# A two-layer decoder trunk on one core: the second stage dealt out to 24 slots, keys opened while their item is projected

## The chip, the cores and the metric

The kernel runs on one core of one Trainium2 chip. The metric is the device time of one execution in microseconds (us). An engine's name stands for itself: PE (matrix multiply), DVE (vector), ACT (scalar), POOL (GpSimd), SP (issues DMAs).

## The reference, cut to what matters

The second stage of the kernel is the gated DeltaNet of layer 0: a projection, a short causal convolution with SiLU, and a chunked delta rule over 8 heads. Sixteen meta tokens form a chunk of their own ahead of 2048 real tokens.

```python
proj = rmsnorm(h, norm_g) @ w_in
qkv = silu(causal_depthwise_conv(proj[..., :QKV_W], conv_w));  z = proj[..., QKV_W:...]
q, k = l2norm(q) * dk ** -0.5, l2norm(k)          # 8 heads, 128 wide
# per chunk of c tokens (16 meta tokens, then chunks)
tmat = eye(c) + where(strict, beta * (k @ k.T) * gam, 0)
u, w = triangular_solve(tmat, [v * beta, k * beta * exp(gcum)])
qk = (q @ k.T) * gam
def step(s, ...):                                  # one chunk after the other
    v_new = u_c - w_c @ s
    o_c = qd_c @ s + qk_c @ v_new
    s = s * dl_c + kd_c.T @ v_new
o = rmsnorm(o, o_norm) * silu(z);  return o @ w_out
```

Output projection, shared keys and values, the window attention of layer 1 and the final norm follow in the third and fourth stage, which the change doesn't touch.

## The kernel before

The program has four stages, one behind the other. The second, `gated_deltanet`, works on 32 **items**: 4 groups of 512 tokens times 8 heads. Items 0 to 7 also carry their head's meta chunk (a second `Pass`, of one chunk, ahead of the main one of four). It runs as a software pipeline of 34 **steps**. In step `it` PE projects item `it`; the passes `a` of item `it - 1` are **opened**; the passes `b` of item `it - 2` are **closed**. Steps 32 and 33 have nothing to project.

The names that the text uses:

- *Projection*: 8 units of 24 matmuls (two halves of 264 tokens, for keys, values, queries, gate in this order: `f` = 0 to 3), 192 in a step. The fp32 product is made of three fp32r ones, so each weight is split: ACT writes the high part (`split_high`), POOL the low part (`split_low`). ACT copies each unit out of PSUM (`evacuate`), DVE convolves it in four taps and bounds it (`convolve`, parts 0 to 4), ACT forms the sigmoid in three activations, POOL multiplies (`silu`) into `kT`, `vT`, `qT`, `zT`.
- *Opening*: `tok` transposes keys, queries and values (12 transposes on PE, L1103); `kk` and `kq` are the products; ACT squares and takes logarithms for the norms; DVE writes `k_dec`, `nU` (the strictly lower part), `v_s`, `qk`.
- *The rows*: DVE inverts the 16x16 diagonal blocks of `nU` row by row (`solve_row`, i = 1 to 15; a product and a reduction each, then the copy `p_Xbt`). The blocks come and go through DRAM: SP stores `nU` (`low_dram`), loads the blocks (`p_blk`); behind row 15 it stores 8 block tiles (L641) and loads the whole inverse `p_X`, `p_Xt` (L647, L649).
- *Levels*: `left` 0 to 2 and `right` 0 to 2 on PE, with DVE and ACT between, join the blocks to the inverse of 128x128. `left` 0 waits for the loaded inverse.
- *Recurrence*: `ks`, `wr`, `out` for each of 4 chunks, a chain PE, DVE (`p_r`), PE, ACT (`p_w`), PE, DVE (`p_state`).
- *Norm and close*: mean square on DVE, logarithm and scale on ACT (`p_on`, L808), four transposes on PE (L1188), product on DVE (`p_og`), a store.

`schedule` deals all that to **slots**, the same list on all engines. In a slot an engine first does its stages and then its share of projection, taps, sigmoids, splits or rows. Before, the list of a step with one pass each is: `tok`, `kk`, `left` 0, `right` 0, `kq`, `left` 1, `right` 1, `left` 2, `right` 2, the twelve of the recurrence, `norm`, `close`: 23 slots, all with about 8 or 9 projection matmuls. Weights are split as their units end. Every engine runs its own list in order and waits on semaphores. PE's `tok` has three waits, of which the first is for the SiLU of the queries:

```python
pe.wait_ge(silu_done, NF * p.item + 3)
```

The 8 PSUM banks are two for the projection and `k`, `v`, `l`, `t`, `c`, `q`. The outputs of the recurrence stand in `t` and `l`, which the levels use too, so `left` 0 of the next item waits until they are read.

## Time and profile before

| | us |
|---|---|
| median of 3 runs | 3182.96 (3181.33 to 3186.96) |
| the profiled execution | 3186.96 |
| its span, first to last instruction | 3185.1 |
| PE busy | 2614.5 (82%) |
| DVE busy | 1619.3 (51%) |
| ACT busy | 1227.2 (39%) |
| POOL busy | 864.6 (27%) |

The page has busy times over the whole span; the second stage's matmuls are L1083 to L1188, and its first projection matmul starts at 137.2. Items follow each other at a constant pace in a long stretch, so the windows and timelines below are cut at their borders. A number in square brackets behind a row is the time for which the engine sat idle before it, and what released it.

### The profile page before, as it was taken

What the parts mean: (1) busy time and instruction counts of PE and PEld (TensorE: products, weight loads), DVE (VectorE), ACT (ScalarE), POOL (GpSimd) and SP (SyncE); (2) the same over time, 40 slices, a digit from 0 to 9 for tenths busy, and PEclk for the clock granted to TensorE, in tenths of its full rate; (3) what the DMA queues carried; (4) which work ended last, traced back from release to release, by engine and by line L of the source; (5) the groups of instructions that cost most, each with busy time, mean ns of one, the idle gap of its engine ahead of it and who ended that gap; (6) DMA issues with size and microseconds to landing.
All of it is one profiled execution on the core that took longest, in us unless ns stands there. A gap on an engine that the chain in (4) does not pass through costs nothing. (4 is left out here: it accounts for less than half of the span.)

```text
span 3185.1 us, 51348 instructions
## 1 busy us (share of the span) xinstructions
PE 2614.5 (82%) x17497; PEld 2330.2 (73%) x17497; DVE 1619.3 (51%) x3652; ACT 1227.2 (39%) x3466; POOL 864.6 (27%) x700
## 2 busy tenths in 40 slices
PE   5577777878787878788787755999995899999997
PEld 4477777778787878777787734888883687888785
DVE  4367676565665656565666523222223444444442
ACT  4244444444444444444444323333332323323232
POOL 0143333333333333333333200000001233223231
PEclk8689998988898889898898757999997999999998
DMA  9632222322223322222222133333334222122111
GB/s 250 184 123 65 72 68 72 115 69 65 70 63 93 99 71 62 72 69 73 70 64 75 35 97 126 129 126 115 112 116 154 86 75 74 60 66 72 61 61 42
DMA packets 250075, 284.27 MB, mean 89 GB/s; under 512 B 72082, under 2 KB 188770, under 8 KB 249986
## 3 DMA queue, kind: packets, MB, share of 16 engines
q1 hardware_dynamic: 208866, 257.73, 26.2%
q10 hardware_dynamic: 41120, 25.37, 2.7%
q8 instruction: 54, 0.88, 0.1%
q14 instruction: 35, 0.29, 0.0%
HBM read 199.71 MB, written 83.33 MB: 89 GB/s over the span
## 5 line engine op out<-in xcount | busy, mean ns | idle before, releaser
L1083 PE MATMUL p_psp<-xg,p_whi 128*128 128x264 f32 x4096 | 890.3, 305 | 21.3 <-POOL p_wlo L1022 21.3
L1083 PEld LDWEIGHTS p_psp<-xg,p_whi 128*128 128x128 f32 x4096 | 685.7, 199 | 23.9 <-issue 18.3
L1083 PE MATMUL p_psp<-xg,p_wlo 128*128 128x264 f32 x2048 | 618.4, 302 | 0.0
L1022 POOL TENSOR_TENSOR p_wlo<-p_wraw,p_whi 128x512 fp32r<-128x512 f32 x260 | 368.3, 1433 | 300.0 <-ACT p_whi L731 299.9
L1083 PEld LDWEIGHTS p_psp<-xg,p_wlo 128*128 128x128 f32 x2048 | 403.9, 197 | 0.5
L863 DVE SCALAR_TENSOR_TENSOR p_acc<-p_proj,p_taps,p_acc 128x528 f32<-128x528 f32 x288 | 281.5, 977 | 9.2
L2142 PE MATMUL p_psq<-p_wq,p_hT 128*128 128x512 f32 x768 | 216.7, 420 | 38.4 <-DVE p_wq L2083 28.3
L1587 PE MATMUL p_psh<-p_wo,p_o 128*128 128x512 f32 (+1 forms) x816 | 198.1, 402 | 26.0 <-DVE p_wo L1557 22.1
L884 DVE TENSOR_TENSOR p_prod<-p_Xb,p_blk 32x4 f32<-32x4 f32 (+13 forms) x448 | 201.5, 450 | 3.9
L1587 PEld LDWEIGHTS p_psh<-p_wo,p_o 128*128 128x128 f32 (+1 forms) x816 | 150.3, 186 | 67.4 <-issue 19.4
L2142 PEld LDWEIGHTS p_psq<-p_wq,p_hT 128*128 128x128 f32 x768 | 140.5, 196 | 73.3 <-issue 23.2
L742 ACT ACTIVATE p_proj<-p_psp 128x264 f32<-128x264 f32 x256 | 99.5, 389 | 245.0 <-PE p_psp L1083 234.8
L2142 PE MATMUL p_pso<-p_wo,p_oT 128*128 128x512 f32 x768 | 189.6, 400 | 5.1 <-DVE p_oT L2037 5.1
L1569 POOL TENSOR_TENSOR p_o<-p_oraw,p_o 128x1024 fp32r<-128x1024 f32 (+1 forms) x17 | 38.8, 2280 | 508.7 <-ACT p_o L1411 508.7
L1587 PE MATMUL p_psz<-p_wk,p_hT 128*128 128x512 f32 x768 | 176.7, 389 | 0.0
L2142 PEld LDWEIGHTS p_pso<-p_wo,p_oT 128*128 128x128 f32 x768 | 142.5, 190 | 37.1 <-DVE p_oT L2037 8.8
L1103 PE MATMUL p_psk<-p_ident,p_kT 128*128 128x128 f32 x136 | 35.3, 398 | 162.7 <-POOL p_qT L1039 158.2
L1587 PEld LDWEIGHTS p_psz<-p_wk,p_hT 128*128 128x128 f32 x768 | 144.2, 188 | 29.9
L731 ACT ACTIVATE p_whi<-p_wraw 128x512 fp32r<-128x512 f32 x260 | 156.5, 620 | 11.2 <-DVE p_og L981 6.4
L1103 PEld LDWEIGHTS p_psk<-p_ident,p_kT 128*128 128x128 f32 x136 | 22.5, 198 | 171.4 <-issue 99.9
L1890 ACT ACTIVATE p_logits<-p_logits,p_top 128x144 f32<-128x144 f32 x256 | 102.6, 402 | 80.0 <-DVE p_top L1998 79.9
L2246 PEld LDWEIGHTS p_psq<-p_v,p_pT 128*128 128x128 f32 x992 | 119.2, 192 | 16.5 <-issue 11.7
(271 smaller groups left out, 4943.3 us busy)
## 6 DMA issues: line engine op xcount, KB each, us to landing
p_wraw<-w_a_in SPq DMA_DIRECT2D x130, 512.0 KB, 3.7
xg<-xT_dram SPq DMA_DIRECT2D x8, 2112.0 KB, 13.2
hT_dram<-p_hT SPq DMA_DIRECT2D x32, 512.0 KB, 2.9
p_hT<-hT_dram SPq DMA_DIRECT2D x32, 512.0 KB
p_x<-x_in SPq DMA_DIRECT2D x16, 512.0 KB, 4.9
xT_dram<-p_hi ACTq DMA_DIRECT2D x16, 512.0 KB, 6.4
xT_dram<-p_lo ACTq DMA_DIRECT2D x16, 512.0 KB, 7.0
p_grow<-rows_dram SPq DMA_DIRECT2D x32, 256.0 KB, 3.7
```

The lines of the kernel that those rows point to most:

```text
L731: nc.scalar.activation(w_hi[:, slot, cols], w_raw[:, slot, cols], ACT.Copy).then_inc(hi_ready, 1)
L742: nc.scalar.activation(proj[:, f % 2, 3 + half_ * HALF:3 + (half_ + 1) * HALF], ps_p[half_][:, 0:HALF], ACT.Copy).then_inc(proj_read, 1)
L863: nc.vector.scalar_tensor_tensor(a, p[:, part:part + GW], w, a, ALU.mult, ALU.add).then_inc(tap_done, 1)
L884: link(nc.vector.tensor_tensor(t3, x3[:, 0:i, 0:i].rearrange("p j c -> p c j"), b3[:, 0:i, i].unsqueeze(1).to_broadcast([rows, i, i]), ALU ...
L1022: nc.gpsimd.tensor_tensor(w_lo[:, slot, cols], w_raw[:, slot, cols], w_hi[:, slot, cols].bitcast(f32), ALU.subtract).then_inc(lo_ready, 1)
L1083: ins = nc.tensor.matmul(ps_p[half_][:, 0:HALF], (w_hi, w_lo)[i][:, f % 2, kc * P:(kc + 1) * P], xg[:, g % 2, j, kc, half_ * HALF:(half_ + ...
L1103: last = nc.tensor.transpose(ps[:, bank_of[c]], t[:, cols[c]], ident[:])
L1569: nc.gpsimd.tensor_tensor(o_s[1][:, :, 0:rows], o_raw[:, :, 0:rows], o_s[0][:, :, 0:rows].bitcast(f32), ALU.subtract).then_inc(o_lo, 1)
L1587: last = nc.tensor.matmul(out, stationary[i][:, kc, 0:rows], moving(j, kc), start=kc == 0 and n == 0, stop=kc == KC - 1 and n == 2)
L1890: last_ = nc.scalar.activation(logits[:, s_, :], logits[:, s_, :], ACT.Exp, bias=top[:, s_:s_ + 1], accum_out=den[:, s_:s_ + 1])
L2142: ins = nc.tensor.matmul(banks[b][:], stationary[i][:, kc, :], weights[j][:, kc, b * FB:(b + 1) * FB], start=kc == 0 and n == 0, stop=kc = ...
L2246: last_ = nc.tensor.matmul(ps_q[b][:, cols], pT[:, g % 2, x, n * P:(n + 1) * P], v[:, slot, kvh * HD:(kvh + 1) * HD], start=False, stop=g ...
```

## The change

- The step now has three items: `p` (item `it`) has its **keys** opened in the very step in which it is projected: `tokK`, `kk`, `kdec`, `low`, `tokV`, `vs`, and rows 1 to 7 of its solve. `a` (item `it - 1`) gets `tokQ`, `kq`, `qk`, rows 8 to 15 and the levels. `b` (item `it - 2`) gets recurrence, norm, close, and `store` as a stage of its own.
- 24 slots in a fixed order with tables: the recurrence of `b` comes first (slots 0 to 11), the levels of `a` in slots 12 to 17, close in 16. `FILL` gives the projection matmuls of each slot. Meta passes get slots of their own with no fill, ahead of slots 0, 2, 12 and 22.
- PSUM: outputs have two banks of their own (`o0`, `o1`), levels keep `l` and `t`; keys and values share `k`, queries and `kq` go through `l`. The close transposes go into `o0`.
- Weights: `w_hi` and `w_lo` hold all four `f`; `SPLIT` places the splits. `X` becomes one buffer, `cur` too, with the last decay kept in `e_last`; `states` holds 8 heads.
- `tok_ps`, `grown` are split into one semaphore for each operand.

```diff
@@ gated_deltanet
-        w_hi = sb("p2_whi", [P, 2, D], f32r)
+        w_hi = sb("p2_whi", [P, NF, D], f32r)
...
-        o_of = lambda c: (ps_t, ps_l)[c % 2][:, c * P:(c + 1) * P]
+        ps_o = (ps_o0, ps_o1)
+        o_of = lambda p, c: ps_o1[:, P:2 * P] if p.meta else ps_o[c % 2][:, c * P:(c + 1) * P]
+        ps_close = lambda p: ps_o1 if p.meta else ps_o0
...
+        FILL = (8, 9, 6, 8, 9, 8, 4, 10, 8, 8, 10, 8, 3, 2, 3, 5, 2, 9, 12, 12, 13, 13, 9, 13)
+        TAPS = {7: (0, 0, (0, 1)), 8: (0, 0, (2, 3)), 9: (0, 0, (4,)), 16: (0, 1, (0,)), 17: (0, 1, (1,)),
+                18: (0, 1, (2, 3)), 19: (0, 1, (4,)), 20: (0, 2, (0, 1)), 21: (0, 2, (2, 3)), 22: (0, 2, (4,)),
+                1: (1, 3, (4,))}
+        SILU = {11: (0, 0), 21: (0, 1), 0: (1, 2), 3: (1, 3)}
+        SPLIT = {5: (0, 3, 0), 6: (0, 3, 1), 7: (1, 0, 0), 8: (1, 0, 1), 14: (1, 1, 0), 15: (1, 1, 1),
+                 21: (1, 2, 0), 23: (1, 2, 1)}
+        ROWS_P = {19: (1, 2), 20: (3,), 21: (4,), 22: (5, 6), 23: (7,)}
+        ROWS_A = {0: (8, 9), 1: (10,), 2: (11,), 3: (12,), 4: (13,), 5: (14,), 6: (15,)}
...
+            if b:
+                if b[0].meta:
+                    for stage in ("ks", "wr", "out"):
+                        insert(0, (stage, b[0], 0))
...
+                for c in range(TPG):
+                    for n, stage in enumerate(("ks", "wr", "out")):
+                        put(3 * c + n, stage, main, c)
+                put(12, "norm", main, 0)
+                put(16, "close", main, 0)
...
+                for s, stage in ((2, "tokQ"), (6, "kq"), (9, "qk")):
+                    put(s, stage, main, 0)
+                for level in range(LEVELS):
+                    put(12 + 2 * level, "left", main, level)
+                    put(13 + 2 * level, "right", main, level)
...
+                for q in p:
+                    put(10, "gates", q, 0)
+                for s, stage in ((12, "tokK"), (13, "kk"), (13, "kdec"), (14, "low"), (22, "tokV"), (23, "vs")):
+                    put(s, stage, main, 0)
...
+                if stage == "tokK":
+                    pe.wait_ge(silu_done, NF * p.item + 1)
...
                 elif stage == "left":
                     if index == 0:
                         pe.wait_ge(inv_in[par], 32 * (p.turn + 1))
-                        if not (isinstance(b[0].chunk, int) and b[0].chunk == 0):
-                            pe.wait_ge(o_read, b[0].chunk)
+                        pe.wait_ge(qk_ready, k + 1)
...
-                        pe.wait_ge(norm_ready, 2 * k + 1)
+                    pe.wait_ge(q_squared, k + 1)
```

**PE, the border of two steps, before** (L1188 is close, L1103 `tok`; L1083 the projection):

```order
L1188 MATMUL p_psv<-p_ident,p_on 128x128 x4
L1083 MATMUL p_psp<-xg,p_whi 128x264 x2
L1083 MATMUL p_psp<-xg,p_wlo 128x264
L1083 MATMUL p_psp<-xg,p_whi 128x264 x2
L1083 MATMUL p_psp<-xg,p_wlo 128x264
L1083 MATMUL p_psp<-xg,p_whi 128x264 x2
L1083 MATMUL p_psp<-xg,p_wlo 128x264
L1103 MATMUL p_psk<-p_ident,p_kT 128x128 x4
L1103 MATMUL p_psq<-p_ident,p_qT 128x128 x4
L1103 MATMUL p_psv<-p_ident,p_vT 128x128 x4
```

**PE, slots 11 to 14 of the last projecting step, after** (L1205 `left`, L1164 `tokK`, L1222 `right`, L1172 `kk`, L1214 the transposes of `p_X`, L1146 the projection):

```order
L1146 MATMUL p_psp<-xg,p_whi 128x264 x2
L1146 MATMUL p_psp<-xg,p_wlo 128x264
L1205 MATMUL p_psl<-p_X,p_nU 128x64 x4
L1164 MATMUL p_psk<-p_ident,p_kT 128x128 x4
L1146 MATMUL p_psp<-xg,p_whi 128x264 x2
L1146 MATMUL p_psp<-xg,p_wlo 128x264
L1222 MATMUL p_psl<-p_half,p_Xt 128x64 x4
L1172 MATMUL p_psc<-p_kT 128x128 x4
L1146 MATMUL p_psp<-xg,p_whi 128x264 x2
L1205 MATMUL p_psl<-p_X,p_nU 128x64 x4
L1214 MATMUL p_pst<-p_ident,p_X 128x128 x4
L1146 MATMUL p_psp<-xg,p_wlo 128x264
```

The 12 transposes no longer stand together at a step's start; `left` 0 and the keys' transposes of a younger item now follow the recurrence, and the close has moved behind two levels.

**DVE, from row 15 on, before** (the last steps, where no convolution stands between; L888 is the copy that ends the rows, L966 `p_state` of the last chunk, L970 the mean square):

```order
L884 TENSOR_TENSOR p_prod<-p_Xb,p_blk 32x225
L886 TENSOR_REDUCE p_Xb<-p_prod 32x15
L888 COPY p_Xbt<-p_Xb 32x256
L966 SCALAR_TENSOR_TENSOR p_state<-p_state,p_cur,p_psc 128x128
L970 SCALAR_TENSOR_TENSOR p_oms<-p_oss,p_obias 128x4
```

**DVE, the same rows after** (slots 6 to 9 of a step; L952 is the copy):

```order
L1028 TENSOR_TENSOR p_r<-p_psc,p_vs 128x128
L948 TENSOR_TENSOR p_prod<-p_Xb,p_blk 32x225
L950 TENSOR_REDUCE p_Xb<-p_prod 32x15
L952 COPY p_Xbt<-p_Xb 32x256
L925 TENSOR_SCALAR p_acc<-p_proj,p_taps 128x528
L927 SCALAR_TENSOR_TENSOR p_acc<-p_proj,p_taps,p_acc 128x528
L1033 SCALAR_TENSOR_TENSOR p_state<-p_state,p_elast,p_psc 128x128
L927 SCALAR_TENSOR_TENSOR p_acc<-p_proj,p_taps,p_acc 128x528 x2
L1028 TENSOR_TENSOR p_r<-p_psc,p_vs 128x128
```

Row 15 stood ahead of the last chunk's `p_state`, at the end of a step; now it stands behind `p_r` of the third chunk, in slot 6, six slots ahead of the `left` 0 of the same step that needs the inverse.

## Rows read from the trace of the kernel before

**Rows 1.** Windows of PE over the second stage: stretch, us, busy (matmuls), clock, DMA.

```profile
267.30:545.40 278.10, 222.22 (x1690) 0.93 0.24 67
545.40:600.90 55.50, 45.57 (x338) 0.91 0.24 67
600.90:659.20 58.30, 45.53 (x331) 0.88 0.42 137
659.20:712.30 53.10, 41.56 (x320) 0.90 0.24 67
712.30:1020.00 307.70, 249.58 (x1920) 0.89 0.24 69
1020.00:1075.50 55.50, 44.10 (x321) 0.84 0.45 142
1075.50:1791.40 715.90, 579.43 (x4480) 0.90 0.24 68
1791.40:1873.00 81.60, 55.36 (x228) 0.54 0.08 24
```

**Rows 2.** Timeline of PE, item 1233.43 to 1284.57: start, us, matmuls [idle before].

```profile
1233.43 1.12 PE L1103 MATMUL p_psk<-p_ident,p_kT 128*128 128x128 f32 x4 [4.77 <-POOL p_qT L1039]
...
1277.45 0.66 PE L1188 MATMUL p_psv<-p_ident,p_on 128*128 128x128 f32 x4 [4.03 <-ACT p_on L808]
...
1284.57 0.47 PE L1103 MATMUL p_psk<-p_ident,p_kT 128*128 128x128 f32 x1 [4.87 <-POOL p_qT L1039]
```

**Rows 3.** Windows, all engines, the same item: PE, PEld, DVE, ACT, POOL busy; clock.

```profile
1233.43:1284.57 51.14, 41.40 (x320) 39.84 (x321) 32.13 (x79) 23.62 (x69) 19.02 (x15) 0.90 0.24 69
```

**Rows 4.** Windows of PE: the granted clock behind stalls, here and behind one at 328.

```profile
1228.10:1233.40 5.30, 0.57 (x3) 0.50 0.49 148
1233.40:1238.20 4.80, 4.76 (x26) 0.57 0.22 50
328.03:331.00 2.97, 2.97 (x14) 0.50 0.04 11
331.00:333.60 2.60, 2.60 (x17) 0.62 0.68 197
```

**Rows 5.** Timeline of DVE, the same item: the end of its rows.

```profile
1271.75 1.63 DVE L884 TENSOR_TENSOR p_prod<-p_Xb,p_blk 32x225 f32<-32x225 f32 x1
1273.42 0.38 DVE L886 TENSOR_REDUCE p_Xb<-p_prod 32x15 f32<-32x225 f32 x1
1273.83 0.92 DVE L888 COPY p_Xbt<-p_Xb 32x256 f32<-32x256 f32 x1
```

**Rows 6.** Timeline of POOL at that place.

```profile
1271.22 3.30 POOL L1022 TENSOR_TENSOR p_wlo<-p_wraw,p_whi 128x512 fp32r<-128x512 f32 x2
```

**Rows 7.** Timeline of SP, DMA issues behind those rows (x4 are four copies).

```profile
1275.06 1.43 SPq L641 DMA_DIRECT2D inv_dram<-p_Xb  x4
1276.54 1.87 SPq L641 DMA_DIRECT2D inv_dram<-p_Xbt  x4
1280.60 0.39 SPq L647 DMA_DIRECT2D p_X<-inv_dram  x1
1281.03 0.51 SPq L649 DMA_DIRECT2D p_Xt<-inv_dram  x1
```

**Rows 8.** Line 649, the load of the inverse: issue to landing.

```profile
DMA to landing us min/median/max: 3.2/3.4/4.8
```

**Rows 9.** Timeline of DVE in the last steps, where POOL is idle.

```profile
1828.35 0.53 DVE L884 TENSOR_TENSOR p_prod<-p_Xb,p_blk 32x225 f32<-32x225 f32 x1
...
1829.32 0.36 DVE L888 COPY p_Xbt<-p_Xb 32x256 f32<-32x256 f32 x1
```

**Rows 10.** Timeline of PE in the last steps.

```profile
1839.01 1.97 PE L1128 MATMUL p_psl<-p_X,p_nU 128*128 128x64 f32 x8 [5.51 <-DMA p_Xt<-inv_dram]
...
1854.84 0.80 PE L1166 MATMUL p_psc<-p_state,p_kg 128*128 128x128 f32 x2
...
1871.85 1.11 PE L1188 MATMUL p_psv<-p_ident,p_on 128*128 128x128 f32 x4 [2.30 <-ACT p_on L808]
```

More of the change, by code:

```diff
@@ L464, in gated_deltanet @@
         solved = sem("p2_solved")
+        scaled = sem("p2_scaled")
         left_ps = sem("p2_left_ps")
@@ new lines, in last_two, with finish, run @@
+        def last_two(step):
+            for it in (ITEMS - 2, ITEMS - 1):
+                step(it, it % 2, *three(it, it % 2, it // 2, False, False, False), (True, it < ITEMS - 1))
+        def finish(step):
+            _, a, b = three(ITEMS, 0, ITEMS // 2, False, False, False)
+            step(ITEMS, 0, [], a, b, (False, False))
+            step(ITEMS + 1, 1, [], [], passes_of(ITEMS - 1, ITEMS // 2 - 1, 1, False), (False, False))
+        def run(eng, step):
+            start(step)
+            meta_group(eng, step)
+            after_meta(step)
+            later(eng, step, H + 2, ITEMS - 2)
+            last_two(step)
+            finish(step)
@@ L1064, in _, with step @@
+            def step(it, s, p, a, b, splitting):
+                for slot in schedule(it, p, a, b, splitting):
+                    for q, item, f in slot.silu:
+                        silu(q, item, f, b)
+                    for stage, q, index in slot.stages:
+                        stage_of(stage, q, index, b)
+                    for item, f, part in slot.split:
+                        split_low(item, f, part)
             pool.wait_ge(cleared, 1)
-            for f in range(2):
+            for f in range(NF - 1):
```

625 lines of the change are left out of this document (314 added, 311 removed).

## The prediction

> **What bounds the kernel now.** I read the windows of PE over the second stage first, then the timeline of one item, then the engines that PE waits for. Behind the head groups an item takes a constant time: 14 items in 715.9 us, 51.14 each [rows 1]. In the item from 1233.43 to 1284.57 PE is busy for 41.40 us, DVE for 32.13, ACT for 23.62, POOL for 19.02 [rows 3]. PE stands still twice: 4.03 us ahead of the close transposes, for ACT's scaled outputs, and 4.87 us ahead of `tok`, for the SiLU of the queries [rows 2]; shorter waits make up the other 0.8. Behind the first stall the clock falls to 1.2 GHz (granted 0.50), and in the 4.8 us behind the second it is 0.57 [rows 4]. At 0.57 these 4.8 us do 2.7 us of work at 2.4 GHz: a loss of 2.1, and some 0.4 behind the first stall, 2.5 in all. So an item is **38.9 us of PE work at full clock**, 320 matmuls [rows 3] or 0.1216 each, **9.7 us of stalls and 2.5 us of lost clock**. PE is the resource, and what the order of work makes it wait for is the cost.
>
> **The change, part by part.**
>
> *Removed: the two stalls.* Close goes from right behind the recurrence to slot 16. Between stand `left` 0 and 1, `right` 0 and 1, `tokK`, `kk` and the fill 8+3+2+3+5, 69 matmuls, 8.4 us by 0.1216, where 4.03 us are missing: the stall is gone. The queries' SiLU is in slot 0 and is needed in slot 2; ahead of it in the step before, the sigmoid has two slots. I count this as hidden, with the fills of slots 22 to 1 as cover (39 matmuls, 4.7 us); without that cover the 4.87 come back. PE's work itself stays: the same 320 matmuls.
>
> *Added: a closed loop through DRAM within one step.* Row 15 and the copy `p_Xbt` are in slot 6, `left` 0 in slot 12. Before, these two were a step apart, and `left` 0 never waited in the long stretch. The way from the copy's end to a loaded inverse: the copy ends at 1273.83 + 0.92 = 1274.75 [rows 5], 8 stores go out from 1275.06, the last load at 1281.03 [rows 7], and it lands 3.4 us later [rows 8]: 1284.43, so **9.7 us**. Where PE did wait for it, the copy ended at 1829.68 [rows 9] and `left` 0 started at 1839.01 [rows 10]: 9.3 us. SP issues the same copies in the same order, so I keep 9.7.
>
> From the start of slot 6 to the copy's end: `p_r` comes about 0.7 us behind (estimate), then row 15 and the copy. With POOL idle that is 0.53 + 0.38 + 0.36, start to end 1.3 us [rows 9]; beside POOL's splits 1271.75 to 1274.75, 3.0 us [rows 5, 6]. `SPLIT` puts splits into slots 5, 6, 7 and 8, so POOL runs beside the row: 3.7 us rather than 2.0. From slot 6 to slot 12 PE has 76 matmuls (48 of fill, 20 of two chunks, 8 of `kq`): 9.2 us. PE therefore waits ahead of `left` 0 for 3.7 + 9.7 - 9.2 = **4.2 us**, bounds 2.0 + 9.3 - 9.2 = 2.1 and, with DVE a further 1 us late, 5.2. What is queued behind that wait is all of PE: the keys' transposes, `kk`, the levels, and so `nU` and the next rows. A slower projection or keys that come late are hidden under it.
>
> *Kept: part of the clock's loss.* One stall of 4.2 us is left where there were two. Behind the single stall of the meta steps, up to 328.03, the clock is 0.50 for 3 us and 0.62 for 2.6 more [rows 4]: a loss of 1.5 + 1.0 = 2.5. Bounds: nothing, and 3.0. I take 2.2.
>
> *Added: short waits.* `right` 1 and `right` 2 wait for ACT's copy of the transposed `p_X` with 3 and 2 matmuls as cover, the recurrence for DVE, which does the same work in a shorter item: 1.0 in all (today 0.8).
>
> *The larger weight buffers, the banks, the semaphores* move no instruction of their own and cost nothing; the few cycles of `e_last` lie beside PE.
>
> **The sum.** A steady item: 38.9 + 4.2 + 2.2 + 1.0 = **46.3 us**.
>
> - 22 items from 659.2 to 1791.4, 1132.2 us [rows 1]: 22 x 46.3 = 1018.6. The two loads of a token group, which stretched 53.1 and 55.5, move ahead of a step's start; I leave 1.5 us each. Saved 110.6.
> - Five steps with meta passes on all sides, 278.1 [rows 1]: 55.6 each. Their 18 further matmuls (338 against 320) are 2.2 us, and the slots without fill expose a chain of three links and the meta openings, some 4.9 (estimate: a chunk alone takes (1871.85 - 2.30 - 1854.84) / 4 = 3.7 us at the low clock [rows 10], less at the high one, and the openings as much as two links). 53.4 each, saved 11.
> - The two mixed steps, 55.5 and 58.3 [rows 1]: 51.3 and 49, saved 13.5. The first steps: 2.
> - The end, 81.6 us [rows 1]: it has two rounds of levels (15.8 us, 1839.01 to 1854.84) and two recurrences (14.7) one behind the other, a `tok`, and the wait of 5.51 [rows 10]. After: recurrence with `tokQ` and `kq` 17, during which the rows run; inverse at about 20; levels and close 17; recurrence 15; norm and close 5: 57, saved 25.
>
> Together 162 us. The profiled execution took 3186.96: 3025. It lies 4.0 above the median of the runs, so in terms of the median **3020**.
>
> **Rivals.** An item more or less by 1 us moves the whole by 29 us (22 steady and 7 early items).
>
> *The loop is shorter (0.20).* If the row escapes POOL and the clock survives a stall of 2 us, an item is 38.9 + 2.1 + 1.0 = 42: 125 us less, 2895. For it: 1.3 us of rows where POOL is idle [rows 9]. Against: 3.0 us beside splits [rows 5, 6], and the splits stand at that very place.
>
> *DVE becomes the bound (0.17).* Beside the 3.30 us of POOL [rows 6] the last product and the copy took 1.63 and 0.92 instead of 0.53 and 0.36 [rows 5, 9], 1.7 more. If every POOL instruction held DVE for its whole length, DVE would need 32.1 - 1.7 + 19.0 = 49.4 us an item [rows 3]: 3.1 x 29 = 90 us more than forecast, 3110. For it: less slack to dodge in. Against: over the item today DVE has 19 us free. The Trainium skill, page "SBUF — State Buffer", section "SBUF: two separate sides", says just this: the port pair of DVE and GpSimd is an exclusive lock, held for a whole instruction, and the other fully blocks. By that rule an item is 49.4; the row bears it out for two instructions, not for the 19 us.
>
> *Slower than before (0.06).* One place: `tokK`, behind `left` 0, needs the keys' SiLU of slot 11, which waits for DVE's bound in slot 9, three sigmoid activations, and the two gates activations that wait for DVE in slot 10. By my order it is ready about as `left` 0 ends. If DVE enters slot 7 late, this is late by as much, and each microsecond costs 29. From an item of 51.9 on (5.6 us beyond the forecast) the change loses; at 53, 3215.
>
> *No effect (0.02).* The same matmuls, stalls merely moved: within 0.2% needs 51.7 to 52.1.
>
> **How the numbers follow.** My case has 0.55, with a range of its own of 2975 to 3070 (items from 44.7 to 48). With the short loop and the DVE case at its edges the range is 2895 to 3110. Faster by over 0.2% (about what a measurement of this kernel can tell): 0.92; within: 0.02; slower: 0.06.
>
> **What would show it.** In the profile after: no wait ahead of the close transposes; a wait of PE for the DMA of `p_Xt` ahead of `left` 0, some 4 us in most items; the copy's end to `left` 0 about 9.7 us; a clock below 1 only behind it; items about 46 us apart. The forecast is wrong if PE waits for POOL's `p_kT` or for `p_r` instead, or if `left` 0 doesn't wait.

## The result and the profile after

The changed kernel took 3134.98 us (median of 4 runs, 3124.81 to 3141.46) beside 3184.96 of the kernel before on the same chip: a ratio of 0.984, 95% interval 0.981 to 0.987. It is faster by 50 us (1.6%), where 162 were forecast. The profiled execution took 3139.08 us.

The page of the changed kernel: span, busy times, and the groups of the second stage that this is about (busy us, mean ns).

```profile
span 3137.1 us, 51318 instructions
...
PE 2621.3 (84%) x17497; PEld 2322.6 (74%) x17497; DVE 1693.4 (54%) x3692; ACT 1219.9 (39%) x3462; POOL 848.5 (27%) x693
...
L1080 POOL TENSOR_TENSOR p_wlo<-p_wraw,p_whi 128x512 fp32r<-128x512 f32 x256 | 358.2, 1411 | 519.9 <-ACT p_whi L790 519.4
```

DVE has gone from 1619.3 to 1693.4 us with almost no work added (the small copies `p_elast`): that is the first thing to see. Windows of PE over eleven steady items, then of all engines over one of them (answers to [rows 1] and [rows 3]):

```profile
1118.47:1658.73 540.26, 451.89 (x3493) 0.96 0.24 72
...
1166.30:1217.06 50.76, 42.66 (x322) 40.80 (x321) 36.01 (x80) 23.30 (x69) 18.41 (x15) 0.93 0.23 69
```

The eleven items take 49.1 us each (50.8 and 47.9 in turn, now and then a third size). Over all 22 items from close to close, 673.62 to 1758.12, it is 49.3. PE stands still for 88.4 us of the eleven, 8.0 each. With the 38.9 us of work of the prediction 2.2 of the 49.1 are left, the lost clock. The forecast was 38.9 + 5.2 + 2.2: **the waits are what was wrong**. Whom PE waits for, the stretch from 1000 to 1700 (14.2 items; us in total, times, longest):

```profile
PE p_psc L1256 <- DVE p_r L1028: 41.9, 29, 3.1
PE p_psc L1247 <- DVE p_state L1033: 27.1, 25, 1.2
PE p_psk L1164 <- POOL p_kT L1099: 27.0, 14, 2.1
PE p_psl L1225 <- ACT p_Xt L853: 7.5, 14, 0.5
PE p_psl L1222 <- ACT p_Xt L853: 5.8, 14, 0.4
...
PE p_psl L1205 <- DMA p_Xt<-inv_dram: 0.3, 1, 0.3
```

Both old stalls [rows 2] are gone, as forecast (for the queries 0.2 us an item is left). The wait for the DMA ahead of `left` 0, forecast as 4.2 us in most items, happened once, for 0.3 us. In its place stand waits for DVE, 69 us in all, and for the keys' SiLU, 27. The costliest one, PE first, then DVE, then POOL, at the border of two steps:

```profile
1185.10 0.49 PE L1256 MATMUL p_psc<-p_r,p_Xt 128*128 128x128 f32 x2 [3.08 <-DVE p_r L1028]
...
1182.35 0.19 DVE L950 TENSOR_REDUCE p_Xb<-p_prod 32x7 f32<-32x49 f32 x1
1183.27 1.25 DVE L1055 COPY p_taps<-p_convw 128x12 f32 x1 [0.72 <-DVE p_Xb L950]
1184.76 0.29 DVE L1028 TENSOR_TENSOR p_r<-p_psc,p_vs 128x128 f32<-128x128 f32 x1 [0.24 <-DVE p_taps L1055]
1184.97 0.88 DVE L948 TENSOR_TENSOR p_prod<-p_Xb,p_blk 32x64 f32<-32x64 f32 x1
...
1183.23 1.26 POOL L1080 TENSOR_TENSOR p_wlo<-p_wraw,p_whi 128x512 fp32r<-128x512 f32 x1 [4.83 <-ACT p_whi L790]
```

A copy of twelve columns takes 1.25 us, as long as POOL's subtraction of 512 that began 0.04 us before it; in the items where no POOL instruction meets it it is 0.17. PE's matmul waits 3.08 us for the `p_r` behind it, where it waits 1.52 in the item before (at 1135.71), in which the copy meets nothing: the hold of 1.08 us and a longer idle time ahead of the copy (0.72 us for 0.29) make up that difference, and the other 1.5 us is there in either item. The copy is met in 6 of the 14 items from 1000 to 1700. PE's clock is low after the long wait. Windows of PE, the stall and the 4.4 us behind it:

```profile
1182.30:1184.90 2.60, 0.00 (x0) 1.00 0.00 0
1184.90:1189.30 4.40, 4.20 (x22) 0.62 0.33 119
```

The way through DRAM, which the forecast had as the bound (DVE's copy, SP's issues, PE's `left` 0):

```profile
1196.18 0.97 DVE L952 COPY p_Xbt<-p_Xb 32x256 f32<-32x256 f32 x1
...
1197.19 1.40 SPq L707 DMA_DIRECT2D inv_dram<-p_Xb  x4
...
1201.70 0.51 SPq L716 DMA_DIRECT2D p_Xt<-inv_dram  x1
...
1205.70 0.67 PE L1205 MATMUL p_psl<-p_X,p_nU 128*128 128x64 f32 x5
```

The copy is lengthened as forecast, 0.97 (0.92 in [rows 5]), but from its end, 1197.15, to the last load's landing, 3.3 us (the median of that line) behind 1201.70, it is 7.85 us and not 9.7, and PE takes until 1205.70 to get to `left` 0 with its waits on the way. Most of the difference lies between the first store and the last load: 1197.19 to 1201.70, 4.5 us, for 6.0 in [rows 7].

### The profile page after: what moved, and what is told of

Read it like the earlier page. It is cut to its first block and busy times, and to the rows that moved or that the text cites. A ratio compares the mean times of both kernels' runs of the same rounds, so it can differ in the third digit from the quotient of the medians.

```text
span 3137.1 us, 51318 instructions
## 1 busy us (share of the span) xinstructions
PE 2621.3 (84%) x17497; PEld 2322.6 (74%) x17497; DVE 1693.4 (54%) x3692; ACT 1219.9 (39%) x3462; POOL 848.5 (27%) x693
## 3 DMA queue, kind: packets, MB, share of 16 engines
q1 hardware_dynamic: 208722, 256.75, 25.5%
## 5 line engine op out<-in xcount | busy, mean ns | idle before, releaser
L1146 PE MATMUL p_psp<-xg,p_whi 128*128 128x264 f32 x4096 | 845.3, 297 | 19.7 <-POOL p_wlo L1080 19.7
L1146 PEld LDWEIGHTS p_psp<-xg,p_whi 128*128 128x128 f32 x4096 | 666.1, 194 | 22.2 <-issue 20.1
L1146 PE MATMUL p_psp<-xg,p_wlo 128*128 128x264 f32 x2048 | 609.3, 298 | 0.0
L1080 POOL TENSOR_TENSOR p_wlo<-p_wraw,p_whi 128x512 fp32r<-128x512 f32 x256 | 358.2, 1411 | 519.9 <-ACT p_whi L790 519.4
L1146 PEld LDWEIGHTS p_psp<-xg,p_wlo 128*128 128x128 f32 x2048 | 396.0, 193 | 0.0
L948 DVE TENSOR_TENSOR p_prod<-p_Xb,p_blk 32x4 f32<-32x4 f32 (+13 forms) x448 | 220.7, 493 | 4.5
L809 ACT ACTIVATE p_sig<-p_sig 128x528 f32<-128x528 f32 x128 | 82.5, 645 | 358.7 <-DVE p_sig L929 358.7
L1970 ACT ACTIVATE p_out<-p_h 128x1024 f32<-128x1024 f32 x16 | 16.9, 1058 | 279.1 <-DVE p_h L2109 279.1
```

What stands on the lines that cost most here:

```text
L809: ins = nc.scalar.activation(v, v, ACT.Exp, scale=-1.0)
L948: link(nc.vector.tensor_tensor(t3, x3[:, 0:i, 0:i].rearrange("p j c -> p c j"), b3[:, 0:i, i].unsqueeze(1).to_broadcast([rows, i, i]), ALU ...
L1080: nc.gpsimd.tensor_tensor(w_lo[:, f, cols], w_raw[:, f % 2, cols], w_hi[:, f, cols].bitcast(f32), ALU.subtract).then_inc(lo_ready, 1)
L1146: ins = nc.tensor.matmul(ps_p[half_][:, 0:HALF], (w_hi, w_lo)[i][:, f, kc * P:(kc + 1) * P], xg[:, g % 2, j, kc, half_ * HALF:(half_ + 1) ...
```

## The experiments

Theories, named as in the expectations. *1*: DVE's work, stretched by POOL's beside it, holds PE up. *2*: the way through DRAM does. *3*: ScalarE's gates and keys do. *4*: the edge of the loop over pairs of items costs time. Ratios are to the kernel before, beside which each ran on the same chip; differences in us are to the 3135 of the changed kernel unless said otherwise. The changed kernel's own interval is 10 us wide to either side, so a difference of less than some 12 us from it can't be told from nothing.

### Which of the four: a_narrow, b_halftaps, h_noinv, g_unroll

```diff
-                cols = slice(part * D // 2, (part + 1) * D // 2)
+                wide = D // 2 if isinstance(it, int) and it == 0 else 32
+                cols = slice(part * D // 2, part * D // 2 + wide)
```

> GpSimd's subtraction for the low parts of the weights writes 32 of each 512 columns (for all items but the first), so this run leaves out most of the weights' low parts; nothing else of the program is changed. Theory 1 (VectorE bounds the steady item, and its instructions are stretched while GpSimd works beside them): the stretched products and taps of slots 20 to 9 fall back to their lengths when alone, 3 to 5 us of an item; items of 45 to 47 us instead of 49.4 and a time of 3000 to 3060 us. Theory 2 (the way of the solved blocks through DRAM bounds the item): the DMAs are as before, within 0.5 us an item, 3115 to 3150 us. Theory 3 (the gates and the keys on ScalarE bound it): the same as theory 2.

Measured: 3010.43 us, 0.946 (0.944 to 0.947): 125 us less. DVE's groups from 1000 to 1700 in a_narrow:

```profile
L927 DVE SCALAR_TENSOR_TENSOR p_acc<-p_proj,p_taps,p_acc 128x528 f32<-128x528 f32 x126 | 97.9, 777 | 4.0
L948 DVE TENSOR_TENSOR p_prod<-p_Xb,p_blk 32x81 f32<-32x81 f32 (+6 forms) x203 | 92.5, 456 | 2.0
...
L925 DVE TENSOR_SCALAR p_acc<-p_proj,p_taps 128x528 f32<-128x528 f32 x42 | 20.5, 489 | 16.3 <-ACT p_proj L801 15.7
```

and the same groups in the changed kernel:

```profile
L927 DVE SCALAR_TENSOR_TENSOR p_acc<-p_proj,p_taps,p_acc 128x528 f32<-128x528 f32 x129 | 119.8, 929 | 4.3
L948 DVE TENSOR_TENSOR p_prod<-p_Xb,p_blk 32x4 f32<-32x4 f32 (+6 forms) x196 | 106.7, 545 | 1.9
...
L925 DVE TENSOR_SCALAR p_acc<-p_proj,p_taps 128x528 f32<-128x528 f32 x43 | 37.6, 875 | 16.2 <-ACT p_proj L801 15.7
```

Not one DVE instruction was edited, and the taps, the first taps and the rows' products took 152, 386 and 89 ns less each.

```diff
-...scalar_tensor_tensor(a, p[:, part:part + GW], w, a, ALU.mult, ALU.add)
+...scalar_tensor_tensor(a[:, 0:HALF], p[:, part:part + HALF], w, a[:, 0:HALF], ALU.mult, ALU.add)
```

> Taps 1 to 3 of the three convolutions run over half of their columns, so this run leaves out half of the convolution; nine VectorE instructions an item fall from about 0.9 us to about 0.5 us, 3.5 us of its work, some 2 us of it in the stretch of slots 20 to 1 in which VectorE is back to back. Theory 1 (VectorE bounds): items of 46 to 47.5 us instead of 49.4, 3040 to 3085 us. Theory 2 (the way through DRAM bounds) : the rows start a little sooner and the loop is shorter by at most 1 us, 3105 to 3140 us. Theory 3 (gates and keys on ScalarE): nothing, 3125 to 3145 us.

Measured: 3100.49 us, 0.974 (0.972 to 0.976): 35 us less, between the two forecasts. DVE's own work counts, some half as much as theory 1 asked. PE's waits for `p_r` fall from 41.9 to 21.5 us of the 700.

```diff
-                sp.wait_ge(inv_out, 16 * stored_blocks(p))
-                sp.dma_start(X[:], square(inv_d[0])[:, 0:TPG, :])...
+                if not zero(p.item):
+                    sp.wait_ge(inv_ready, p.item)
+                unit = lambda n: consts["ident"].unsqueeze(1).to_broadcast([P, n, P])
+                sp.dma_start(X[:], unit(TPG)).then_inc(inv_in[p.par], 16)
```

(and the same for `Xt`; the stores follow it).

> The matrices X and Xt that the levels start from are loaded from the identity as soon as the levels of the item before are over, ahead of the stores of the solved blocks: this run leaves the solved blocks out of the result, and the levels no longer wait for solve, store and load. Instructions on all engines and the count of DMAs stay. Theory 2 (this way through DRAM bounds the item): the item is freed of it and falls to what TensorE needs, 42 to 46 us, 2900 to 3040 us. Theory 1 (VectorE bounds): the load was there when slot 12 asked for it, and the item moves by less than 0.5 us, 3120 to 3145 us.

Measured: 3135.27 us, 0.984 (0.982 to 0.986), the changed kernel's time. **Theory 2 has fallen** for this kernel: with the inverse off the path nothing moves. (Where the other waits shrink, the DMA's comes up behind them; see the end of the experiments.)

```diff
-            with eng.Fori(first // 2, end // 2) as j:
+            for j in range(first // 2, end // 2):
```

(and the same in `meta_group`).

> The two loops over pairs of items are written out, with the same instructions in the same order, so that no loop edge and no address worked out in registers is left. Theory 4 (the long and the short items, 50.8 and 47.9 us, differ by the edge of the loop, which holds all engines up): both are 47.9 us or less, 3090 us or less, by 1.5 us on each item. Theory 1 (VectorE's work bounds both): within 0.5 us an item, 3120 to 3150 us, and the difference of odd and even items stays. Instructions fetched once each instead of out of a loop could cost time instead; then the waits at a slot's start show it on all engines.

Measured: 3115.79 us, 0.978 (0.976 to 0.980): 19 us less. The items are 48.7 and 47.1 us in turn in the first half of the stretch, 50.3 and 48.7 in the second: the edge costs something, less than the 1.5 us an item of theory 4. The copy `p_taps` is 0.17 us in each of its 14 items here: without the 0.72 us ahead of it, it runs before POOL's subtraction.

### Moving the work: f_splits, d_early, c_acttap, cd

```diff
-        SPLIT = {5: (0, 3, 0), 6: (0, 3, 1), 7: (1, 0, 0), 8: (1, 0, 1), 14: (1, 1, 0), 15: (1, 1, 1),
+        SPLIT = {12: (0, 3, 0), 13: (0, 3, 1), 14: (1, 0, 0), 15: (1, 0, 1), 17: (1, 1, 0), 18: (1, 1, 1),
```

(and SP's load of the raw weights of the queries goes behind the load of the blocks).

> The four halves of a weight split that stand in slots 5 to 8, beside VectorE's rows and taps, and the two of slots 14 and 15 go to slots 12 to 15, 17 and 18, where VectorE waits for TensorE between the levels; the raw weights' and lower triangles' DMAs are put in the order in which they then come due. Same work, nothing left out. Theory 1 (VectorE's work, stretched by GpSimd beside it, bounds the item): with all eight halves narrowed the stretch was 3.6 us an item; four of eight out of the busy stretch give back about half, 1.5 to 2 us an item, 3075 to 3095 us. Rival 1a (what counts is that GpSimd's own queue is late, with its keys and its SiLU behind the splits): in slots 12 to 18 the splits then stand ahead of tokK and the keys for the next item, and nothing or less than nothing is won, 3125 to 3160 us. Rival 1b (the stretch moves with the splits onto the levels' half and X, which are on the way of the levels): 3110 to 3150 us.

Measured: 3104.19 us, 0.974 (0.971 to 0.977): 31 us less, where theory 1 had 40 to 60 and both rivals less than 25. DVE's first taps are back at 490 ns (875 in the changed kernel) and the copy `p_Xbt` at 0.37 us (0.97), but the other taps went up, from 929 to 1014 ns. `left` 0 now waits for the DMA of the inverse in all 14 items, 0.5 us each.

```diff
-        TAPS = {7: (0, 0, (0, 1)), 8: (0, 0, (2, 3)), 9: (0, 0, (4,)), 16: (0, 1, (0,)), 17: (0, 1, (1,)),
-                18: (0, 1, (2, 3)), 19: (0, 1, (4,)), ...
+        TAPS = {7: (0, 0, (0, 1)), 8: (0, 0, (2, 3)), 9: (0, 0, (4,)), 13: (0, 1, (0,)), 14: (0, 1, (1,)), 15: (0, 1, (2,)),
+                16: (0, 1, (3,)), 17: (0, 1, (4,)), ...
```

(with its sigmoid in 17 and 18 and its SiLU in 19).

> The taps, the sigmoid and the SiLU of the second function go from slots 16 to 21 to slots 13 to 19, into VectorE's idle stretches between the levels. Same work. Theory 1: VectorE's back to back stretch begins at slot 20, where its predecessor's taps are over already, so that at most 1 us an item is won, and the taps now stand ahead of the levels' half and X, which TensorE waits for: between 3100 and 3150 us. If VectorE's work alone counted, wherever it lies, nothing would change at all: 3125 to 3145 us.

Measured: 3152.43 us, 0.989 (0.986 to 0.991), 17 us more. DVE's taps in d_early, from 1000 to 1700:

```profile
L927 DVE SCALAR_TENSOR_TENSOR p_acc<-p_proj,p_taps,p_acc 128x528 f32<-128x528 f32 x126 | 146.1, 1159 | 4.2
```

1159 ns against 929: in slots 14 and 15 they now stand beside two splits. So work put into DVE's idle time was stretched there. But PE doesn't stand still longer for it: its waits for `p_r` and `p_state` fell from 69.0 to 57.0 us of the 700, new ones for `p_half` and `p_X` of the levels came (14.8), and over ten steady items (1124.40 to 1630.20) it stands still 7.9 us an item, as in the changed kernel. What is lost is clock: PE is busy 42.7 us an item for the same 320 matmuls, where it was 41.1.

```diff
-                    nc.vector.tensor_scalar(a, p[:, 0:GW], w, None, ALU.mult).then_inc(tap_done, 1)
+                    # on ScalarE, behind the evacuation of the second half
+                    nc.scalar.activation(acc[:, f % 2, :], proj[:, f % 2, 0:GW], ACT.Copy,
+                                         scale=taps[:, 4 * f:4 * f + 1]).then_inc(tap_done, 1)
```

> The first of the four taps of each of the three convolutions (a product with one number for each partition) goes from VectorE, 764 ns each in the changed kernel and three an item, to ScalarE as an activation with a scale, about 0.6 us each. Same computation. Theory 1 (VectorE bounds): 2.3 us of VectorE's work an item is gone, of which about two thirds lie in its busy stretch: 1.2 to 2 us an item, 3075 to 3100 us. Theory 3 (ScalarE's gates and keys bound the item): the three added activations stand ahead of the sigmoids and the gates, 1 to 2 us longer an item, 3160 to 3190 us.

Measured: 3144.11 us, 0.986 (0.984 to 0.987): 9 us more, not to be told from the changed kernel, and neither theory's number. Three DVE instructions an item are gone and no time with them. The rest of the taps went from 929 to 1044 ns and POOL's product `p_vT` from 1291 to 1778: the meeting with POOL passed on to the next instruction. That is not all of it: DVE now waits for the activations (25.2 us of the 700 ahead of the second taps, for 15.7 ahead of the first taps before), and PE's waits for DVE's `p_r` and `p_state` fell from 69.0 to 52.3 while one for POOL's `p_vT`, 17.5, is new. How much of that wait is POOL's and how much ScalarE's, this run doesn't separate.

> The last two together: first taps on ScalarE and the second function's taps, sigmoid and SiLU in slots 13 to 19. Theory 1: as c_acttap alone or up to 20 us less, 3060 to 3100 us. Theory 3: slower than the changed kernel, over 3150 us.

Measured (both edits): 3149.20 us, 0.987 (0.984 to 0.989). As d_early alone, within what can be told.

### Taking POOL's work away: k_dvelow, kf, m_nopool, fg

```diff
-                nc.gpsimd.tensor_tensor(w_lo[:, f, cols], w_raw[:, f % 2, cols], w_hi[:, f, cols].bitcast(f32), ...
+                nc.vector.tensor_tensor(w_lo[:, f, cols], w_raw[:, f % 2, cols], w_hi[:, f, cols].bitcast(f32), ...
```

> The eight subtractions of an item that give the low parts of the weights go from GpSimd (1.39 us each in the changed kernel) to VectorE, in the same slots; the same computation, and VectorE has eight instructions more of some 0.7 us each (estimate from the taps' 0.78 us without GpSimd beside them, 528 columns of two tiles). Theory 1, as an exclusion (the two engines take turns at their operands, so that the sum of what both have to do counts): the sum of VectorE's 29.3 us an item (456 us in 15.6 items with the splits narrowed) and GpSimd's 19 falls by 8 x (1.1 to 1.4 - 0.7) = 3 to 5 us, and items are 45 to 47 us, 2990 to 3060 us. Rival (VectorE is bound by its own work, and the stretching is a surcharge of 3.6 us an item as a_narrow shows it): 5.6 us of work come and 3.6 of stretch go, 2 us more an item, 3170 to 3210 us.

Measured: 3149.87 us, 0.989 (0.987 to 0.991): 15 us more, wrong for both. What is left of the meeting stands right ahead of PE's longest wait. The copy at the step's start and PE's waits, from 1000 to 1700:

```profile
L1062 DVE COPY p_taps<-p_convw 128x12 f32 (+1 forms) x14 | 17.2, 1227 | 0.0
```
```profile
PE p_psc L1256 <- DVE p_r L1035: 63.1, 28, 4.1
```

One such place, DVE, POOL and PE, and a window of PE behind it:

```profile
1134.60 1.36 DVE L916 TENSOR_TENSOR p_wlo<-p_wraw,p_whi 128x512 fp32r<-128x512 f32 x1 [0.65 <-ACT p_whi L790]
1135.88 1.23 DVE L1062 COPY p_taps<-p_convw 128x12 f32 x1
...
1135.57 1.51 POOL L1120 TENSOR_TENSOR p_qd<-p_qT,p_er 128x512 f32<-128x512 f32 x1 [0.16 <-POOL p_qT L1104]
...
1137.65 0.80 PE L1256 MATMUL p_psc<-p_r,p_Xt 128*128 128x128 f32 x2 [4.12 <-DVE p_r L1035]
...
1137.00:1143.60 6.60, 5.95 (x27) 0.50 0.27 79
```

With the split of slot 23 on DVE, the copy comes later, and in every item beside POOL's product `p_qd`. It takes 1.23 us instead of 0.17, the subtraction ahead of it 1.36 (0.68 in m_nopool) beside POOL's SiLU of the queries, and PE waits 4.5 us an item for `p_r` (63.1 in 13.9 items), where it was 2.9. But `p_state` gave back as much (5.2 us of the 700 for 27.1), so that the two waits together are what they were, 68.3 for 69.0. The loss is again in the clock: one long wait instead of several short ones, and behind the one of 4.12 us the granted clock is at its lower level, 0.50, for 6.6 us. PE stands still 8.0 us an item and is busy 42.2, where it was 8.0 and 41.1.

kf is k_dvelow with the table of f_splits.

> The subtractions on VectorE and six of the eight halves in slots 12 to 18 (the edit of f_splits). Exclusion: as k_dvelow, and another 1 us an item since the work stands where VectorE waits: 2960 to 3040 us. If the subtractions stand in the way of the levels' half and X instead, it is over k_dvelow by 1 to 2 us an item. Surcharge: 3130 to 3170 us.

Measured: 3185.14 us, 1.000 (0.999 to 1.001): 50 us more, wrong for both. DVE waits 48.4 us of the 700 for ACT's high parts, in its own order, ahead of what the levels need. On POOL the same wait held up nothing of DVE's. But that is not where the 50 us are: PE stands still less than in the changed kernel, 7.3 us an item for 8.0. It is busy for 44.5 us an item instead of 41.1 with the same matmuls, at a mean granted clock of 0.89 from 1000 to 1700 (0.96 in the changed kernel). The copy is held here too, 1.23 us in all 13 items, and the waits for `p_r` are as long as in k_dvelow (up to 4.1 us). Why the clock falls so much more often than there no run isolates.

m_nopool moves the SiLU products, kg and qd as well:

```diff
+                    for q, item, f in slot.silu:              # in VectorE's step, behind the slot's rows
+                        silu(q, item, f, b)
+                    for stage, q, index in slot.stages:
+                        grow(stage, q, index, b)              # kg in tokK, qd in tokQ
```

> All that GpSimd does in the second stage, the eight subtractions, the four SiLU products, kg and qd, goes to VectorE, in the same slots, behind the slot's rows and taps; the same computation, GpSimd idle. VectorE has 29.3 + 14 x 0.7 = 39 us of work an item and TensorE 38.9 at full clock. Exclusion: the sum of both engines falls from 48 to 39 us, and items are 43 to 46 us, 2900 to 3030 us. Surcharge alone: VectorE 39 us in place of 35.8 with GpSimd beside it, 3200 to 3240 us. A third way: VectorE now waits in its own order for ScalarE's sigmoids ahead of each product, which could add 1 to 3 us an item to either.

Measured: 3048.78 us, 0.956 (0.955 to 0.958): **86 us less, with 14 instructions an item more on DVE** and none of them on another engine. Windows of all engines from 1000 to 1700 (the changed kernel has 507.77 for DVE there), and DVE's groups:

```profile
1000.00:1700.00 700.00, 614.28 (x4864) 584.18 (x4863) 546.69 (x1435) 353.90 (x1053) 0.00 (x0) 0.98 0.24 72
```
```profile
L969 DVE SCALAR_TENSOR_TENSOR p_acc<-p_proj,p_taps,p_acc 128x528 f32<-128x528 f32 x135 | 103.2, 765 | 4.3
L916 DVE TENSOR_TENSOR p_wlo<-p_wraw,p_whi 128x512 fp32r<-128x512 f32 x115 | 78.7, 684 | 11.7 <-ACT p_whi L790 9.7 <-DVE p_Xb L992 1.0
L990 DVE TENSOR_TENSOR p_prod<-p_Xb,p_blk 32x49 f32<-32x49 f32 (+6 forms) x219 | 65.6, 300 | 1.6
```

The rows' products are at 300 ns (545 in the changed kernel), the subtraction costs 0.68 us where POOL took 1.39. The item is 45.8 us. PE stands still 5.6 us of it, 2.5 less than in the changed kernel, so that a good part of its waits is there without POOL as well: 1.8 us for the values' SiLU, 1.2 for the keys', 1.3 for `p_r` and `p_state`, 0.9 for `p_Xt`. The time is 19 us over the range of the exclusion and far from the 3200 of the surcharge.

fg is f_splits with g_unroll's loops.

> The splits' new slots (f_splits) with the loops written out (g_unroll). If the two gains have separate causes they add: 31 and 19 us under the changed kernel's 3135, so 3075 to 3095 us. If both remove the same wait, 3100 us.

Measured: 3063.22 us, 0.961 (0.959 to 0.963), 41 us under f_splits: more than the sum of the two gains (72 us for 50).

### Is it the lock: r_busy, r_levels, n_hybrid, mg

m_nopool with four POOL instructions an item whose result nobody reads:

```diff
+                    for item, f, part in slot.split:          # r_busy
+                        if f in (0, 3):
+                            pool.wait_ge(hi_ready, 2 * (NF * item + f) + (part + 1))
+                            link(nc.gpsimd.tensor_tensor(spare[:, 0, :], spare[:, 1, :], spare[:, 2, :], ALU.subtract))
...
+                    for level in range(2):                    # r_levels
+                        pool.wait_ge(left_ps, LEVELS * a[-1].item + level + 1)
+                        for _ in range(2):
+                            link(nc.gpsimd.tensor_tensor(spare[:, 0, :], spare[:, 1, :], spare[:, 2, :], ALU.subtract))
```

> On top of m_nopool (3049 us, GpSimd idle in the second stage) GpSimd subtracts two spare tiles of 128x512 four times an item, in slots 5 to 8 beside VectorE's rows and taps, and nothing waits for the outcome. Lock: each of the four holds up a VectorE instruction whose operands lie in SBUF, by 0.6 to 1.2 us, on the way of rows and taps: 1.5 to 4 us an item, 3090 to 3165 us. If GpSimd's work cost time only by its results' coming late: nothing, 3040 to 3060 us.

Measured: 3146.10 us, 0.988 (0.986 to 0.990): 97 us over m_nopool. DVE and POOL in r_busy, the end of the rows (compare [rows 5, 6, 9]):

```profile
1108.13 1.43 DVE L992 TENSOR_TENSOR p_prod<-p_Xb,p_blk 32x225 f32<-32x225 f32 x1
1109.59 0.38 DVE L994 TENSOR_REDUCE p_Xb<-p_prod 32x15 f32<-32x225 f32 x1
1110.00 1.27 DVE L996 COPY p_Xbt<-p_Xb 32x256 f32<-32x256 f32 x1
...
1107.61 1.52 POOL L1144 TENSOR_TENSOR p_spare<-p_spare 128x512 f32<-128x512 f32 x1 [0.16 <-POOL p_spare L1144]
1109.75 1.28 POOL L1144 TENSOR_TENSOR p_spare<-p_spare 128x512 f32<-128x512 f32 x1 [0.61 <-ACT p_whi L792]
```

In m_nopool these three take 0.55, 0.38 and 0.38 us. Here product and copy end 0.43 and 0.24 us behind POOL's instruction, and the reduction between them keeps its length. Nothing depends on POOL, so its results cannot be late: **the two engines' meeting alone costs these 97 us**. PE's waits for `p_state` went from 10.2 to 49.0 us of the 700.

> The same four idle subtractions an item, but started by the first and second `left` of the levels, in slots 12 to 16, where VectorE mostly reads PSUM (half, X, kdec, nU) or waits. Lock by operands: a few SBUF-only instructions (copies of small tiles, the splits of slots 14 and 15) are held up, at most 1 us an item, 3045 to 3085 us. Lock of every VectorE instruction whatever it reads: as r_busy or more, since these instructions stand on the way of the levels.

Measured: 3163.70 us, 0.994 (0.992 to 0.996): 115 us over m_nopool, where at most 36 were expected. The reads of PSUM kept their lengths, as expected (`p_half` and `p_X` 0.42 us, `p_nU` 0.35). But the SiLU of the keys took 1.26 us instead of 0.69, PE's wait for it grew from 1.29 to 1.95 us, and behind that the clock fell. PE in r_levels, ahead of and behind its waits for the keys (1.95 us, to 1103.87) and the values (1.86, to 1127.45):

```profile
1099.00:1103.00 4.00, 2.67 (x22) 1.00 0.93 307
1106.00:1111.00 5.00, 5.00 (x25) 0.50 0.00 0
1123.00:1127.00 4.00, 2.59 (x22) 1.00 0.00 0
1127.50:1131.50 4.00, 4.00 (x22) 0.60 0.00 0
```

and at the same two places in m_nopool, behind waits of 1.29 and 1.87 us:

```profile
1119.00:1123.00 4.00, 3.59 (x33) 1.00 0.00 0
...
1136.20:1140.20 4.00, 3.97 (x34) 1.00 0.00 0
```

Over the steady items (1114.30 to 1619.40, and 1123.40 to 1627.70 in m_nopool) the item is 50.5 us for 45.8: PE stands still 6.9 us of it instead of 5.6, and is busy 43.6 instead of 40.3. Of the 4.7 us, 1.3 are waits and 3.3 the clock. 1.6 us of the clock's loss (4 us at 0.60) stand behind the values' wait, which had not grown, so what the added 0.7 us of the keys' wait costs by itself isn't shown.

n_hybrid, cut to the two conditions that share out the splits:

```diff
+                        if f == 2:          # VectorE, which also has the SiLU products and qd: slots 21 and 23
...
+                        if f != 2:          # POOL, which also keeps kg: slots 12 to 18
```

> f_splits with the work divided by place: GpSimd keeps kg of slot 12 and the six subtractions of slots 12 to 18, beside VectorE's reads of PSUM; VectorE takes the SiLU products, qd and the two subtractions of slots 21 and 23. The same computation. Lock by operands: VectorE has 14 x 0.7 less 7 x 0.7 = 4.9 us less than in m_nopool's 39 and is hardly held up: items of 43.5 to 45.5 us instead of 45.9, 2975 to 3045 us. If the lock holds whatever VectorE reads: 3060 to 3110 us.

Measured: 3047.18 us, 0.956 (0.955 to 0.958), the same as m_nopool, 2 us over the range. The rows' products are at 0.30 us and `p_Xbt` at 0.37, so POOL's seven instructions beside the levels cost DVE little (the copies of `p_state` and `p_elast`, 1.09 and 0.62 instead of 0.21 and 0.16), but PE now waits 3.2 us an item for the values' SiLU (1.8 in m_nopool), and 0.7 for the DMA of the inverse.

mg is m_nopool with g_unroll's loops.

> m_nopool with the two loops written out. If the loop's edge is a cost of its own, it gives 19 us here as it did alone: 3020 to 3040 us. If it only let VectorE catch up, nothing: 3040 to 3055 us.

Measured: 3010.70 us, 0.945 (0.943 to 0.946): 38 us under m_nopool, twice what was expected.

### The edit that lost, with POOL silent: mgd, and ng

mgd is mg with the tables of d_early, ng is n_hybrid with g_unroll's loops.

> mg (3011 us: all of GpSimd's work on VectorE, loops written out) with the edit of d_early: taps, sigmoid and SiLU of the second function some four slots earlier. In m_nopool TensorE waits 1.9 us an item for the values' SiLU ahead of tokV. If d_early lost to the lock (its taps stood beside the splits of slots 14 and 15), this wait now goes: 1 to 2 us an item, 2955 to 2985 us. If its taps stood in the way of the levels, GpSimd or not, the time is over 3011: 3015 to 3035 us.

Measured: 2985.77 us, 0.937 (0.936 to 0.939): 25 us under mg, 1 us over the expected range. Nearly all items are 44.1 or 44.2 us. DVE's taps from 1000 to 1700:

```profile
L969 DVE SCALAR_TENSOR_TENSOR p_acc<-p_proj,p_taps,p_acc 128x528 f32<-128x528 f32 x129 | 98.9, 767 | 3.0
```

767 ns, where the same edit beside POOL had 1159. PE's wait for the values' SiLU, 23.9 us of the 700 in mg, is gone, the one for `p_r` is 25.5 instead of 9.3. The same tables lose 17 us beside POOL and gain 25 without it, so the place was good and POOL's work beside it made the loss. (The two pairs also differ in the loops; d_early with the loops written out was not run.)

> n_hybrid (3047 us) with the loops written out. As the edit gave 19, 41 and 38 us in three other kernels: 3005 to 3030 us. n_hybrid waits 3.4 us an item ahead of tokV for the values' SiLU; if that wait stays, the loop's edge was not on its path and it is 3035 to 3050 us.

Measured: 3034.51 us, 0.952 (0.950 to 0.954): 13 us under n_hybrid, between the two. The wait for the values' SiLU stays (44.4 us of the 700), and the one for the inverse grows:

```profile
PE p_psl L1240 <- DMA p_Xt<-inv_dram: 15.8, 16, 4.5
```

That is 1.0 us an item, once 4.5: the closed loop of the prediction, which is nothing in the changed kernel, becomes a limit once DVE and POOL are out of the way.

**mgd beats both kernels**: 6.3% less than before, 4.8% less than the changed one.

Waits and clock side by side, from close to close over the steady items (us an item, with the same 320 matmuls in each):

| | window | items | item | PE still | PE busy | clock |
|---|---|---|---|---|---|---|
| changed kernel | 1118.47 to 1658.73 | 11 | 49.1 | 8.0 | 41.1 | 0.96 |
| a_narrow | 1117.90 to 1612.20 | 11 | 44.9 | 4.5 | 40.4 | 0.98 |
| d_early | 1124.40 to 1630.20 | 10 | 50.6 | 7.9 | 42.7 | 0.94 |
| k_dvelow | 1117.80 to 1619.50 | 10 | 50.2 | 8.0 | 42.2 | 0.94 |
| kf | 1128.50 to 1595.00 | 9 | 51.8 | 7.3 | 44.5 | 0.89 |
| m_nopool | 1123.40 to 1627.70 | 11 | 45.8 | 5.6 | 40.3 | 0.98 |
| r_busy | 1080.70 to 1622.40 | 11 | 49.2 | 7.7 | 41.6 | 0.95 |
| r_levels | 1114.30 to 1619.40 | 10 | 50.5 | 6.9 | 43.6 | 0.91 |
| mg | 1096.00 to 1631.90 | 12 | 44.7 | 5.1 | 39.6 | 1.00 |
| mgd | 947.00 to 1521.10 | 13 | 44.2 | 4.8 | 39.4 | 1.00 |

What d_early, k_dvelow and kf lose against the changed kernel is all in the time that PE is busy, and so in the clock. Taking POOL's work away gains in both, waits and clock. And in none of these kernels are the waits under 4.5 us.

## Why the prediction was wrong

- *The two stalls are gone*: right. Nothing is left of the wait ahead of the close, and 0.2 us an item of that for the queries.
- *The closed loop through DRAM*: wrong, 4.2 us were forecast and 0.3 us happened once. From the copy's end it is 7.85 us instead of the 9.7 of [rows 7, 8], and h_noinv shows that without it nothing changes. The turn between first store and last load was 4.5 us and not 6.0; why, no run tells.
- *Short waits, 1.0 us*: **this is the term that failed**. They are 8.0 us: 4.9 an item for DVE's `p_r` and `p_state` (69.0 in 14.2 items), 1.9 for POOL's keys, 0.9 for ACT's `p_Xt`, 0.3 others. The prediction had taken DVE and POOL as meeting at one place, row 15, and had read [rows 5, 6] as its price. But in the traces they meet in products, copies and taps all over the item, and the change put rows, taps and the recurrence of three items side by side, so that DVE is late for the next link of a chain that PE waits for. DVE is busy 36.0 us in the item of 1166.30 against 32.13 [rows 3] for the same work. The meeting is not all of the missing 7.0 us: with POOL's work narrowed or gone 4.5 to 5.6 us of waits are left (a_narrow, m_nopool, mgd), for the keys', the values' and the recurrence's links. So the lock is some 2.5 to 3.5 us of it; the rest stands ahead of links that the prediction had priced at 1.0 in all, and no run takes it apart.
- *The lost clock, 2.2 us*: about right in size, wrong in place: it stands behind the waits for `p_r` and for the keys (0.50 from 1186.1 to 1189.3 and from 1209.9 to 1213.1). The size is partly luck, for the 38.9 us of work that it is counted from is too small: in mg and mgd, where the granted clock is 1.00 throughout, the same 320 matmuls keep PE busy for 39.6 and 39.4 us. By that the changed kernel loses some 1.6 us, and the kernel before lost 1.9 and not 2.5.
- *The sum*: cut at the first projection matmul of a step (the first one at 138.8), the changed kernel's second stage against the forecast is: the 22 items 1084.0 us for 1021.6 with the group loads, 62 more; the five meta steps 290.3 (58.1 each) for 267, 23 more; the two mixed steps 101.3 for 100.3; the end, from the last projection matmul, 1772.13, to the last close, 1825.80 + 1.11, 54.8 for 57, which was right. What the prediction passed over are **the first three steps**: 157.7 us, where it had the 130.1 of before less 2. That is 30 us, a quarter of the whole miss. In them PE waits 7.1, 7.3 and 3.7 us for the keys of its own step (`p_kT`), and in each meta step 3.7 for the keys and 2.6 ahead of `tokV`: a step that opens the keys it has just projected waits for their SiLU, and the prediction had these waits as hidden under the one for the DMA. Together it is 114 us, from the forecast 3025 to the 3139 of the profiled execution.
- *The rival "DVE becomes the bound"* gave 49.4 us an item, and 49.3 was measured. That the two agree is luck. It had 0.17, and the kernel's time, 3135, lies beyond the 3110 it set, since the first and the meta steps were slower too. The Trainium skill, page "SBUF — State Buffer", section "SBUF: two separate sides", calls the port pair of DVE and GpSimd an exclusive lock, and gives it to DVE only for an operation in a 2-port mode, or for one with two inputs in SBUF against a GpSimd operation that reads SBUF. r_busy agrees: 1.43 us for a product of 0.55, ended 0.43 us behind POOL's instruction, and the reduction between product and copy, with one input, kept its 0.38. (In which mode DVE's copies and first taps ran, which were held too, no trace shows.) The prediction's condition, that every POOL instruction holds DVE for its whole length, is wider than the page's. And what does not hold in the traces is that the sum of both engines' work sets the item. In a_narrow DVE's 456 and POOL's 141 us fill 597 of 700, and in m_nopool DVE's 547 do: neither engine is full. What counts is which DVE instruction is met and who waits for it: k_dvelow, with POOL busy for 108 of the 700 us instead of 260, was no faster, with a subtraction and a copy of twelve columns held ahead of PE's longest wait.
- *What would show it*: the prediction named `p_kT` and `p_r` as the waits that would prove it wrong, and these they were.

Shown is that POOL's instructions lengthen DVE's (a_narrow, r_busy) and that DVE's lateness makes PE wait; and that waits of the same sum, placed otherwise, can cost clock on top (k_dvelow, kf). Open are the waits that are left without POOL, what makes the clock fall behind one wait and not behind another, and what the edge of the loop does: written out it gave 19, 41, 38 and 13 us in four kernels. In the changed kernel DVE stood idle 0.72 us there and met POOL behind it; with POOL silent it gave even more, so the meeting is not its whole cost.
